# Order of the expert blocks on TensorE: small experts in runs of two to four behind every second large block, instead of one or two behind each

## The reference

```python
def swiglu(x, w_gate, w_up, w_down):
    return (jax.nn.silu(x @ w_gate) * (x @ w_up)) @ w_down

def moe_swiglu(x, w_router, w_gate, w_up, w_down):
    logits = (x @ w_router).astype(jnp.float32)
    top_v, top_i = lax.top_k(logits, TOP_K)
    gates = jax.nn.softmax(top_v, axis=-1)
    combine = jnp.sum(jax.nn.one_hot(top_i, N_EXPERTS, dtype=jnp.float32) * gates[..., None], axis=-2)
    out = jnp.zeros_like(x)
    for e in range(N_EXPERTS):
        out = out + combine[..., e:e + 1].astype(x.dtype) * swiglu(x, w_gate[e], w_up[e], w_down[e])
    return out
```

## Time and profile before

| | us |
|---|---|
| median of 3 runs (lowest to highest) | 1157.72 (1156.75 to 1159.4) |
| the profiled execution | 1161.09 |
| its span, first to last instruction | 1159.2 |
| PE busy | 1115.8 (96%) |
| DVE busy | 642.5 (55%) |
| ACT busy | 467.4 (40%) |
| DMA, in 500 to 1120 us | 355 GB/s |

### The profile page before, as it was taken

The page is one execution under the profiler, slowest core; times in us unless marked ns, Lnnn a source line. Parts: engine busy times, 40 slices in busy tenths (PEclk is TensorE's granted clock), DMA queues, the critical chain, the costliest instruction groups (busy, mean ns, idle before and its releaser), DMA issues.

```text
span 1159.2 us, 14644 instructions
## 1 busy us (share of the span) xinstructions
PE 1115.8 (96%) x5874; PEld 824.1 (71%) x5874; DVE 642.5 (55%) x742; ACT 467.4 (40%) x593; POOL 44.2 (4%) x45
## 2 busy tenths in 40 slices
PE   7899999999999999989999999999999999999995
PEld 6677878888877778776666676666666666666663
DVE  3787675545467876754655534554543465555334
ACT  4465543344335656143444423333333334433220
POOL 2000020000023000000000000000000000000001
PEclk9999999999999999889999999999999999999998
DMA  9933256555547500088999989899999989999952
GB/s 284 366 127 109 77 181 210 186 181 181 181 145 216 210 1 1 1 314 325 358 370 353 347 331 371 296 394 386 337 371 342 374 293 383 372 356 336 395 213 76
DMA packets 126781, 300.07 MB, mean 259 GB/s; under 512 B 4938, under 2 KB 7128, under 8 KB 126704
## 3 DMA queue, kind: packets, MB, share of 16 engines
q1 hardware_dynamic: 124304, 291.52, 69.4%
q0 software_dynamic: 2112, 6.87, 2.2%
q10 hardware_dynamic: 288, 0.63, 0.1%
HBM read 297.88 MB, written 1.12 MB: 258 GB/s over the span
## 4 chain that ended last, share of the span: by engine, by line
PE 87%; DMA 6%; DVE 3%; ACT 2%; issue 2%; SPq 0%; POOLq 0%; POOL 0%; DVEq 0%; ACTq 0%
PE bank L1517 23%; PE bank L1518 22%; PE bank L1575 12%; PE bank L1945 7%; PE bank L1603 6%; DMA raw<-in_w_in 3%; PE bank L1955 3%; PE bank L1682 3%; PE bank L1791 2%; PE bank L1776 1%; PE bank L1708 1%; PE bank L1925 1%; DMA raw<-in_moe_w_up 1%; ACT w_hi L712 1%; DMA raw<-in_moe_w_down 1%
## 5 line engine op out<-in xcount | busy, mean ns | idle before, releaser
L1371 DVE TENSOR_TENSOR w_lo<-raw,w_hi 128x2048 fp32r<-128x2048 f32 x84 | 192.5, 2292 | 278.5 <-ACT w_hi L877 278.5
L1517 PE MATMUL bank<-w_hi,xT_hi 128*128 128x512 f32 (+1 forms) x832 | 333.4, 402 | 10.3 <-ACT w_hi L877 3.3
L1518 PE MATMUL bank<-w_hi,xT_lo 128*128 128x512 f32 (+1 forms) x832 | 323.2, 390 | 0.0
L877 ACT ACTIVATE w_hi<-raw 128x2048 fp32r<-128x2048 f32 x84 | 160.6, 1912 | 246.6 <-PE bank L1575 140.4
L1517 PEld LDWEIGHTS bank<-w_hi,xT_hi 128*128 128x128 f32 x832 | 158.1, 190 | 78.6 <-issue 34.5
L991 DVE TENSOR_TENSOR w_lo<-raw,w_hi 128x2048 fp32r<-128x2048 f32 x63 | 144.2, 2290 | 108.7 <-ACT w_hi L712 108.4
L1518 PEld LDWEIGHTS bank<-w_hi,xT_lo 128*128 128x128 f32 x832 | 158.4, 190 | 29.3
L1575 PE MATMUL bank<-w_lo,xT_hi 128*128 128x512 f32 (+1 forms) x640 | 168.2, 386 | 0.0
L712 ACT ACTIVATE w_hi<-raw 128x2048 fp32r<-128x2048 f32 x65 | 124.6, 1918 | 102.4 <-PE bank L1575 45.9
L1575 PEld LDWEIGHTS bank<-w_lo,xT_hi 128*128 128x128 f32 x640 | 118.8, 189 | 24.4
L1517 PE MATMUL bank<-w_hi,hT_hi 128*128 128x512 f32 x312 | 124.6, 399 | 2.3 <-issue 2.3
(11 more groups left out here) (202 smaller groups left out, 1022.7 us busy)
## 6 DMA issues: line engine op xcount, KB each, us to landing
raw<-in_moe_w_gate SPq DMA_DIRECT2D x70, 1024.0 KB, 8.4
raw<-in_moe_w_up SPq DMA_DIRECT2D x70, 1024.0 KB, 8.6
raw<-in_moe_w_down SPq DMA_DIRECT2D x70, 1024.0 KB, 8.3
raw<-in_w_in SPq DMA_DIRECT2D x24, 1024.0 KB, 9.0
raw<-in_ffn_w_gate SPq DMA_DIRECT2D x11, 1024.0 KB, 5.1
raw<-in_ffn_w_up SPq DMA_DIRECT2D x11, 1024.0 KB, 5.1
raw<-in_ffn_w_down SPq DMA_DIRECT2D x11, 1024.0 KB, 4.9
raw<-in_w_out SPq DMA_DIRECT2D x8, 1024.0 KB, 5.9
```

Source lines behind the costliest of these rows:

```text
L877: nc.scalar.activation(w_hi[:, m % NH, :], raw[:, n % NR, :], ACT.Copy).then_inc(hi_done, 1)
L1371: nc.vector.tensor_tensor(w_lo[:, m % NH, :], raw[:, (BASE_MOE + load[at[o]]) % NR, :], w_hi[:, m % NH, :].bitcast(F32), ALU.subtract).the ...
L1517: nc.tensor.matmul(o, hi, wh, start=start, stop=False)
L1518: nc.tensor.matmul(o, lo, wh, start=False, stop=False)
```

## The change

`interleaved` now puts nothing behind the first, third, fifth ... large block, and behind every second one a run of small blocks, up to `RUN` = 4, as long as the small ones are short of their share; a run ends early behind a small expert's last up block and its last down block, as it did before.

```diff
+RUN = 4
-    order, done, pause = [], 0, False
+    order, done = [], 0
     for k, unit in enumerate(larges):
         order.append(unit)
-        if unit[2:4] == ("down", N_DOWN - 2):
+        if k % 2 == 0:
             continue
-        if pause:
-            pause = False
-            continue
-        due = len(smalls) * (k - 1) / (len(larges) - 6)
-        for _ in range(2):
-            if done < min(due, len(smalls)) and not pause:
-                order.append(smalls[done])
-                pause = smalls[done][2:] in (("up", NCH - 1, 1), ("down", N_DOWN - 1, 0))
-                done += 1
+        due = min(len(smalls) * (k + 1) / (len(larges) - 6), len(smalls))
+        run = 0
+        while done < due and run < RUN:
+            order.append(smalls[done])
+            done, run = done + 1, run + 1
+            if smalls[done - 1][2:] in (("up", NCH - 1, 1), ("down", N_DOWN - 1, 0)):
+                break
     assert done == len(smalls)
     return order
```

## The result

The changed kernel takes 1169.21 us (median of six, 1163.12 to 1171.29) against 1157.24 us for the kernel before (six, 1155.05 to 1159.4): a ratio of 1.0094, interval 1.0063 to 1.0125. It is slower by about 11 us, where 1159.9 was forecast, with 1153.5 to 1168 as the range. It lies above the range. The two intervals meet between 1.0063 and 1.0092; all twelve executions average 1166.9 us, and 86 executions of the kernel before average 1157.2. So I take 9.7 us as what has to be explained.

What follows compares the result with a forecast made beforehand. TensorE's own work, 87% of the chain, was taken as the bound. Gains of 14.3 us against costs of 16.5 gave net +2.2 us, moving the median from 1157.72 to 1159.9 us, range 1153.5 to 1168.

Steps and rivals of the forecast that it cites:

- The order's sum: Expert stage: gains from fewer runs and vanished waits against new waits and late transfers, clock left out; +1.2 us.
- 33 runs fewer: TensorE in the expert stage: 72 runs of small blocks become 39, at 0.35 us each, 11.6 us less.
- waits that go: TensorE's two 0.43 us waits at first down blocks and two transfer waits (1.8 us) vanish: together 2.7 us less.
- g4.0 of S0, S1, S2: g4.0 waits for DVE's first addition of chunk 3, needing g3.1 of the same run: 3.7, 2.1, 2.1 us.
- u0.1 of S1 and S2: In their first runs u0.1 waits for DVE's addition of the last scatter product: 1.5 us, twice.
- first run of S0: Now directly behind the gather: g0.0 starts 0.7 us late, u0.1's transfer adds 0.5 us; sum 1.2 us.
- transfers, S2's d7 among them: Small blocks landing late: 1.9 us for S2's run of four at d4 to d7, 1.5 us at runs of three.
- clock: TensorE's granted clock falls after idle waits such as S0's 3.7 us: 1 us taken, 0 to 3.4.
- Slower by the clock: Rival: each of three TensorE waits of 2.1 to 3.7 us brings a 1.2 GHz stretch; 1166 us; chance 0.15.
- Slower by transfers: Rival: runs of four return buffers late, so last blocks land late, 12 + 5 us; 1173 us; chance 0.15.
- Faster by shorter waits: Rival: only half of the 10.9 us of waits comes and transfers are in time; 1150 us; chance 0.15.
- What I said would show it wrong: Profile signs: no idle before g4.0, many DMA releasers, or clock under 1.00 at several places between 520 and 1120 us.

Runs made afterwards that it cites:

- again: The changed kernel, unchanged, timed a second time beside the kernel before: 1164.52 us, ratio 1.0069.
- gather: Changed kernel with the gathers of S1 and S2 moved whole behind the next large block, out of the run of small blocks: 1169.35 us, ratio 1.0093.
- aftersplit: Changed kernel with the gathers of S1 and S2 in two halves behind the next two large blocks, waits left idle: 1168.45 us, ratio 1.0088.
- afterhalf: Changed kernel with only the first half of each small expert's weights fetched, all TensorE instructions kept: 1157.9 us, ratio 1.0014.
- fill: Changed kernel with full-width products that nobody reads ahead of g4.0 of S0, S1, S2 and u0.1 of S1, S2: 1166.35 us, ratio 1.0066.
- hold: Changed kernel with runs ended ahead of gate blocks needing a sum begun in the run and ahead of u0.1; u1.0 mistakenly still waits: 1176.45 us, ratio 1.0159.
- hold2: Changed kernel with runs ended ahead of every gate or up block needing a sum begun in the same run; still 39 runs: 1161.69 us, ratio 1.0049.
- hold2half: The order of hold2 with only the first half of each small expert's weights fetched: 1146.85 us, ratio 0.9911 to the kernel before.
- beforehalf: Kernel before with only the first half of each small expert's weights fetched: 1158.94 us, ratio 1.0016.
- three: Order of 40 runs, 32 of three and seven of four blocks, none waiting for its own sum, gathers whole: 1157.21 us, ratio 0.9997 to the kernel before.
- fillwide: Changed kernel with waits filled and one unread full-width product behind each of eight steps of S1's and S2's whole gathers: 1164.4 us, ratio 1.0069.
- fillsplit: Changed kernel with the five waits filled and the gathers of S1 and S2 in two halves behind two large blocks: 1162.72 us, ratio 1.0062.
- hold2split: The order of hold2 with the gathers in two halves behind the next two large blocks: 1164.67 us, ratio 1.0051 to the kernel before.

## Why the prediction was wrong

**The order's sum was right.** It said, the clock left out, +1.2 us; the traces say +1.8 and +1.9. That it is so near is in part luck: the runs saved 1.5 us less than the sum had, the first run of S0 and the transfers cost 1.3 us less.

| step | predicted | in the trace of after |
|---|---|---|
| 33 runs fewer | -11.6 | -10.1 (0.31 a run): 640.4 - 14.4 against 638.7 - 2.6 |
| waits that go | -2.7 | -2.6 |
| g4.0 of S0, S1, S2 | 3.7, 2.1, 2.1 | 3.5, 1.9, 2.7 (1.9 by the sum alone) |
| u0.1 of S1 and S2 | 1.5, 1.5 | 1.5, 1.5 |
| first run of S0 | 1.2 | 0.5 |
| transfers, S2's d7 among them | 3.4 (1.9 at d7) | 2.8 (1.4 at d7) |
| clock | 1.0 | 5.7 (`again`: 7.0) |

The waits could be foretold to 0.2 us (but for S2's g4.0 and the first run of S0) since each engine runs in the order written, and before's trace has every piece: where the addition stands behind a split, what it takes, which semaphore holds TensorE.

**The step that failed is the clock's.** I priced it at 1.0 us with 3.4 as its end, from one idle stretch of 3.32 us and one of 1.22 that left the clock up. Two things were wrong in it. The ends were too near: with nothing in the trace between 1.22 and 3.32 us I took the dips at the two waits of 2.1 us as mostly absent. They come in some traces and not in others: behind S1's wait of 1.9 us in `gather` and `aftersplit`, not in after, `again` or `afterhalf`; behind S2's in `again` (2.52 us), `gather` (2.56), `aftersplit` (2.87) and `afterhalf` (1.90), not in after (2.73). The Trainium skill, "TensorE: Matmul & The Clock Gate", section "HAM oscillation — how this bites in real kernels", was cited for exactly that, a loop that pays at each of its gaps; the traces agree at one of the three waits in after, at two in `again`, and at all three in `aftersplit`. And I looked for idle time only. The gather, 32 products of 32 columns, with d4 ahead and d5 to d7 behind it, is one stretch without a wait, 8.0 us at full clock, in which the array is thinly used, and the clock fell in it. Before's order had one block behind the gather where after's has three. I counted the gather as a cover, 3.6 us in which d7 could land, and it was that; nothing in my sum asked what the stretch does to the clock. In place of the 1.0 us the traces show 5.7 and 7.0.

How often a gather brings a dip can be counted over all traces, for S1's and S2's. In after's place (after, `again`, `fill`, `hold`, `hold2`, `hold2half`, `afterhalf`) 10 of 14 have one. In before's place (before, `beforehalf`) 2 of 4 have one, in `three` none of 2. Whole but moved between two large blocks (`gather`), 1 of 2 has one. Halved, none of 10 has one, and widened none of 2. So narrow work is part of the cause, as `fillwide` and `fillsplit` show, but what turns a stretch into a dip in one execution and not in the next is not known.

That both causes are at work, and that either alone keeps most of the loss, is what these five kernels show, by their mean clock:

| | waits idle | waits filled |
|---|---|---|
| gather whole | 0.984 (after and `again`) | 0.984 (`fill`) |
| gather in halves | 0.985 (`aftersplit`) | 0.989 (`fillsplit`) |
| gather whole, widened | not run | 0.990 (`fillwide`) |

Before has 0.989. Taking one cause away moved it by 0.001 and 0.0015, not clear of the standard errors of about 0.001, both by 0.005. At 0.89 us for 0.001 this is 4 to 5 us.

**The rivals.** "Slower by the clock" (0.15, 1166) named the right resource, with one of its two mechanisms, and its 1166 is close to the 1166.9 of all twelve executions. That is partly luck: it counted a dip at each of the three waits, and the two traces have one and two there, and the rest at gathers. "Slower by transfers" fell for the kernel after: 2.8 us of transfer waits outside S2's g4.0, not 17. Its mechanism is true and was only asleep: after's own waits for sums gave the transfers time. Remove them and the bursts cost 11.9 us (`hold2`). "Faster by shorter waits" fell: all five waits came.

**What I said would show it wrong** did: a clock under 1.00 at more than one place between 520 and 1120 us.

**What stays open.** Of the 9.7 us, 1.8 are the order and 4.9 to 6.3 the clock (the first from the mean clock, the second from the half-clock stretches of the two traces, (5.7 + 7.0) / 2). 1.6 to 3.0 us are left. In the orders with many late transfers the stage is longer than its idle time explains, too: for `hold2` 638.7 - 2.6 - 33 x 0.32 + 12.3 = 637.8 against 640.3 in the trace. The runs with half of the small transfers have the same orders, so they show how large this is. Without clock and idle time the stage is 628.0 us in `hold2` against 624.9 in `hold2half`, 626.0 in after against 624.5 in `afterhalf`, and 636.1 in before against 635.5 in `beforehalf`. So full transfers cost TensorE 0.6 to 3.1 us that the traces don't list as idle. By what means is not shown; idle pieces too short to be listed would look like this.

## What to carry to other kernels

Before fewer switches of TensorE's tiling are bought by longer runs, ask three things of each run: does a block in it need a sum that is begun in it, does the transfer queue have the four or five blocks of a period landed in time (look at its busy share in that stage, not only at TensorE's), and how long does the array do narrow work without a full-width block between. End a run ahead of a block that waits for its own run, and keep runs even rather than as long as they go: 40 runs nearly all of three, with the gathers halved, won half of what 33 saved switches are worth (5 of 10.6 us; with whole gathers nothing), where 39 runs with twelve of four and no wait for a sum (`hold2`) lost all of it. When a fix brings nothing, as the filled waits, it may be one of two sufficient causes: try both together before either is dropped.

## What the runs showed of the hardware

- The granted clock also falls in a stretch in which TensorE shows no idle time but does narrow products: 0.66 in 674 to 684 us of after at 10.00 us of 10 busy. It doesn't do so each time (10 of 14 such gathers have a dip, and `beforehalf` has two around shorter stretches). With products of full width among the narrow ones the two gathers of `fillwide` are at 1.00, and none of the ten halved gathers has a dip.
- At half clock three small blocks take 5.35 us in place of 2.78, and large products come 0.43 us apart in place of 0.23.
- An idle wait of 1.9 us lowered it in `aftersplit` (0.83 in the ten us behind), and waits of 1.57 and 1.69 us among narrow blocks did in `hold2split` and `hold2`, though 1.73 us at another place of `hold2` did not, nor 1.22 us in before, 1.49 us at u0.1 of after and 2.73 us at its g4.0. The length of the wait alone doesn't decide it.
- The dips aren't the same in each execution. Mean clocks of the kernel before alone run from 0.984 to 0.994, which is 9 us by their slope.
- Going over to the column tiles of 32 and back costs 0.27 to 0.35 us for a run of one to four blocks, each block counted at 0.88 us (distances of 3.95, 4.83, 5.66 and 6.51 us against 2.72).
